# Moving two weight rests, five semaphore waits and one product order in a two-block fp32 transformer kernel

## The reference, cut to what matters

```python
for i in range(DEPTH):                                   # DEPTH = 2
    hn = rmsnorm(x, norm_mix_w[i])
    x = x + (mlstm_mixer(hn, ...) if i == 0 else window_attn_mixer(hn, ...))
    x = x + swiglu(rmsnorm(x, norm_ffn_w[i]), ffn_w_in[i], ffn_w_out[i])
...
def swiglu(h, w_in, w_out):
    gu = h @ w_in
    gate, up = gu[..., :D_FF], gu[..., D_FF:]
    return (jax.nn.silu(gate) * up) @ w_out
...
# end of window_attn_mixer: 16 query heads, 4 key-value heads
out = out / denom.transpose(0, 1, 4, 2, 3)[..., None]
return out.reshape(B, S, Hq * hd).astype(h.dtype) @ w_out
...
# second block
y_mla = (o_mla * jax.nn.silu(z_mla)) @ w_br_mla[l]
```

## Time and profile before

| | |
|---|---|
| median of 3 runs | 973.01 us (971.74 to 973.33) |
| the profiled execution | 971.56 us, span 969.7 us |
| TensorE busy | 938.5 us, 97% |
| VectorE busy | 584.7 us, 60% |
| ScalarE busy | 478.1 us, 49% |
| mean granted TensorE clock | 0.997 of full speed |
| DMA | 150.30 MB, mean 155 GB/s |

### The profile page before, as it was taken

How to read it: one execution, slowest core, us unless ns; L and a number is a source line. 1 busy time by engine, 2 the same in 40 slices (tenths; PEclk the granted TensorE clock), 3 DMA queues, 4 the chain that set the end, 5 groups by cost and what they waited for, 6 DMA issues and landing times.

```text
span 969.7 us, 13666 instructions
## 1 busy us (share of the span) xinstructions
PE 938.5 (97%) x5035; PEld 778.2 (80%) x5035; DVE 584.7 (60%) x1078; ACT 478.1 (49%) x770; POOL 24.7 (3%) x39
## 2 busy tenths in 40 slices
PE   6999899999999999899999999999999999999996
PEld 6877677888888898777888888889987877888775
DVE  5966857545454688456445454877665556565665
ACT  5556566353443548364353444686344455445442
POOL 0013200000000000000000000000000000000000
PEclk9999999999999999999999999999999999999998
DMA  8551345645546322245644546232423242433441
GB/s 296 213 195 66 134 146 217 223 168 179 210 156 234 131 87 89 87 147 199 233 157 167 222 148 240 90 130 89 173 92 126 87 164 98 174 120 131 167 169 44
DMA packets 25607, 150.30 MB, mean 155 GB/s; under 512 B 3024, under 2 KB 3152, under 8 KB 11344
## 3 DMA queue, kind: packets, MB, share of 16 engines
q1 hardware_dynamic: 24912, 147.44, 41.6%
q0 software_dynamic: 640, 2.11, 0.7%
HBM read 148.50 MB, written 1.05 MB: 154 GB/s over the span
## 4 chain that ended last, share of the span: by engine, by line
PE 83%; DVE 8%; ACT 3%; DMA 2%; issue 1%; DVEq 1%; SPq 0%; ACTq 0%
PE bank L452 24%; PE bank L453 24%; PE bank L454 23%; DVE w_lo L1803 2%; DMA w_raw<-w_main_dram 2%; PE bank L523 2%; PE bank L1008 1%; PE bank L732 1%; DVE arena L2191 1%; PE bank L1023 1%; PE bank L1061 1%; PE bank L1043 1%; PE bank L1044 1%; DVE w_lo L1782 1%; PE bank L845 1%
## 5 line engine op out<-in xcount | busy, mean ns | idle before, releaser
L452 PE MATMUL bank<-w_hi,x_hi 128*128 128x512 f32 (+2 forms) x648 | 262.4, 405 | 1.3 <-DVE w_lo L1717 0.8
L453 PE MATMUL bank<-w_lo,x_hi 128*128 128x512 f32 (+2 forms) x648 | 253.6, 391 | 0.0
L454 PE MATMUL bank<-w_hi,x_lo 128*128 128x512 f32 (+2 forms) x648 | 252.2, 389 | 0.0
L1717 DVE TENSOR_TENSOR w_lo<-w_raw,w_hi 128x2048 fp32r<-128x2048 f32 x50 | 114.6, 2292 | 106.3 <-ACT w_hi L1208 105.5
L1208 ACT ACTIVATE w_hi<-w_raw 128x2048 fp32r<-128x2048 f32 x54 | 103.4, 1917 | 105.9 <-DMA w_raw<-w_main_dram 102.2
L452 PEld LDWEIGHTS bank<-w_hi,x_hi 128*128 128x128 f32 x648 | 122.2, 189 | 32.1 <-issue 5.6
L454 PEld LDWEIGHTS bank<-w_hi,x_lo 128*128 128x128 f32 x648 | 121.7, 188 | 27.3
L453 PEld LDWEIGHTS bank<-w_lo,x_hi 128*128 128x128 f32 x648 | 122.0, 188 | 22.4
L1803 DVE TENSOR_TENSOR w_lo<-w_raw,w_hi 128x2048 fp32r<-128x2048 f32 x51 | 116.2, 2284 | 6.2 <-ACT w_hi L1269 6.1
L1269 ACT ACTIVATE w_hi<-w_raw 128x2048 fp32r<-128x2048 f32 x50 | 94.9, 1908 | 14.8 <-DMA w_raw<-w_main_dram 14.2
L452 PE MATMUL bank<-x_hi,w_hi 128*128 128x256 f32 (+1 forms) x272 | 79.7, 293 | 9.2 <-DVE w_lo L1813 8.9
(11 more groups left out here) (357 smaller groups left out, 1451.8 us busy)
## 6 DMA issues: line engine op xcount, KB each, us to landing
w_raw<-w_main_dram SPq DMA_DIRECT2D x111, 1024.0 KB, 5.4
s_raw<-w_side_dram SPq DMA_DIRECT2D x51, 512.0 KB, 4.2
w_raw<-w_main_dram SPq DMA_DIRECT2D x2, 512.0 KB, 7.1
h<-x_dram SPq DMA_DIRECT2D x2, 512.0 KB, 11.2
arena<-rows_dram POOLq DMA_DIRECT2D x2, 512.0 KB, 4.0
arena<-x_t_dram SPq DMA_DIRECT2D x1, 768.0 KB, 7.8
out_dram<-arena SPq DMA_DIRECT2D x1, 512.0 KB, 2.6
out_dram<-arena SPq DMA_DIRECT2D x2, 256.0 KB, 2.1
```

What stands on the lines that cost most here:

```text
L452: pe.matmul(out, ah, bh, start=first, stop=False)
L453: pe.matmul(out, ah, bl, start=False, stop=False)
L454: return pe.matmul(out, al, bh, start=False, stop=last)
L1717: dve.tensor_tensor(w_lo[:, slot, 4 * g:4 * g + 4, :], w_raw[:, g, :, :], w_hi[:, slot, 4 * g:4 * g + 4, :], ALU.subtract).then_inc(w_lo_o ...
```

## The change

Five edits; no instruction is added or removed but waits.

1. Start of each SwiGLU (TensorE): the wait for the second accumulator stands in front of the first product that writes it, not in front of the transposes of tile 2.
2. Head 20 of the second block (TensorE): half 0 of the rider waits for tiles 0 to 3 only; the wait for all eight stands in front of half 1.
3. Window attention (ScalarE): `w_hi` of chunk 23's second half is made behind tile 3 of the output projection, not behind tile 7.
4. Window attention (VectorE): `w_lo` of chunk 23's first half moves from in front of the third group's normalisation to behind tile 3, the second half from behind tile 7 to behind tile 5.
5. Start of each SwiGLU (VectorE): `w_lo` of the second chunk's second half stands between the two products of row blocks 0 and 1, not behind them. For this `product` calls its argument `between` behind the first.

```diff
@@ def ffn(layer, mixer, next_st), TensorE
-                for r in range(R):
-                    pe.wait_ge(acc_free[(n0 + r) % 2], (n0 + r) // 2)
+                pe.wait_ge(acc_free[n0 % 2], n0 // 2)
                 for k in range(KT - 2):
                     st_wait(f"f{layer}", k)
...
                     for r in range(R):
+                        if (k, r) == (0, 1):
+                            pe.wait_ge(acc_free[(n0 + 1) % 2], (n0 + 1) // 2)
                         first(k, r)
@@ heads of the second block, TensorE
-                if n == min(j for j in range(2 * NH) if RIDERS[j] and RIDERS[j][0][0] == "brm"):
-                    st_wait("o_mla")
+                if n == first_brm:
+                    st_wait("o_mla", KT // 2 - 1)
...
+                if n == first_brm:
+                    st_wait("o_mla")
                 riders(RIDERS[n], 1)
@@ window attention, ScalarE
                     split_st("a_out", lambda k: y_hi[:, k, :], ks=(2 * i, 2 * i + 1))
-            split_half(C_AOUT + 1, (C_AOUT + 1) % 2, 1)
+                    if i == 1:
+                        split_half(C_AOUT + 1, (C_AOUT + 1) % 2, 1)
@@ def ffn, VectorE
-                product(0)
-                rest_second(c0 + 1, (c0 + 1) % 2)
+                product(0, lambda: rest_second(c0 + 1, (c0 + 1) % 2))
@@ window attention, VectorE
-                elif j == 2:
-                    rest_half(C_AOUT + 1, (C_AOUT + 1) % 2, 0)
-            rest_st("a_out", lambda k: y_hi[:, k, :], lambda k: y_lo[:, k, :], ks=range(6))
+            rest_st("a_out", lambda k: y_hi[:, k, :], lambda k: y_lo[:, k, :], ks=range(4))
+            rest_half(C_AOUT + 1, (C_AOUT + 1) % 2, 0)
+            rest_st("a_out", lambda k: y_hi[:, k, :], lambda k: y_lo[:, k, :], ks=(4, 5))
+            rest_half(C_AOUT + 1, (C_AOUT + 1) % 2, 1)
             group_attended(NG - 1)
             rest_st("a_out", lambda k: y_hi[:, k, :], lambda k: y_lo[:, k, :], ks=(6, 7))
-            rest_half(C_AOUT + 1, (C_AOUT + 1) % 2, 1)
```

More of the change, by code:

```diff
@@ L1132, in _ @@
             evacuated(("uv", 2, 0), ("uv", 2, 1))
+            first_brm = RIDERS.index([("brm", 0, 0)])
             for n in range(2 * NH):
```

## The result

| | before | after |
|---|---|---|
| median, timed side by side | 972.75 us (971.74 to 973.33, 4 runs) | 964.27 us (963.32 to 965.36, 4 runs) |
| ratio, with its interval | | 0.9911 (0.990 to 0.9923) |
| profiled execution | 971.56 us, span 969.7 us | 965.36 us, span 963.6 us |

The change saves 8.5 us by the medians and 6.2 us between the two profiled executions. So the first question is not whether the stops went, but why more came back than they held.

What follows compares the result with a forecast made beforehand. TensorE, busy 97% of the span, was taken as the bound, so only its stops could be saved: 3.4 + 1.0 + 1.0 + 0.9 = 6.3 us off the 973.01 us median, predicting 966.7 us, range 965.0 to 969.2 us.

Steps and rivals of the forecast that it cites:

- The clock: Around the 2.4 us stop, 402 to 410 us: granted clock 1.00, so no time at a lower clock can be won back.
- The sum: All closed TensorE stops together: 3.4 + 1.0 + 1.0 + 0.9 = 6.3 us saved.
- Part 3: Second-half `w_lo` wait in each SwiGLU: both 0.49 us waits go, 1.0 us saved, with 0.2 to 0.4 us of cover.
- Part 4: Wait for turned tiles of the first branch, at 821.60 us: the 0.93 us stop is hidden, 0.9 us saved.
- Part 1: Last rests of the window attention: 1.1 us saved at 387 us and 2.3 us at 406 to 408.6, 3.4 us together.
- Part 2: Accumulator wait before each SwiGLU: 0.2 us saved in layer 0, 0.8 us in layer 1, 1.0 us together.
- 1, ScalarE's copy as the releaser: At 388.24 us TensorE waits for ScalarE's copy of head 13, so the first place gives nothing: 967.8 us; chance 0.08.
- 2, savings taken back: In the SwiGLUs, turned tiles and the late second product take savings back: 4.6 us left, 968.4 us; chance 0.14.
- 3 and 4, loads or `w_hi` late: Chunk 24's first half lands after 405: 970 to 973 us, chance 0.04; or chunk 23's `w_hi` late: 975 us, chance 0.02.
- 5, the addition kept by the meta rows: Window attention's end: the meta rows' round trip through ScalarE keeps the first addition late; 4.0 us, 969.0 us; chance 0.04.

Runs made afterwards that it cites:

- Experiment 6: Kernel before with only chunk 23's second-half `w_hi` (ScalarE) and `w_lo` (VectorE) moved earlier in the window attention: 969.04 us, 0.9958, 3.9 us faster.
- experiment 7: Kernel before with nothing moved and 18 useless identity transposes put in TensorE's 2.4 us stop: 971.72 us, 0.9984, 1.2 us faster.
- experiment 12: The kernel before again, nothing changed, for a second profile: 972.88 against 972.93 us, 0.9999.
- experiment 8: Kernel before with only `w_lo` of the second chunk's second half put between the two SwiGLU products, both layers: 971.5 us, 0.9985, 1.45 us faster.
- experiment 4: Kernel before with only TensorE's wait for turned tiles at head 20 of the second block split: 971.76 us, 0.999, 1.2 us faster.
- experiment 5: Kernel before with only VectorE's `w_lo` of chunk 23's first half moved behind tile 3: 971.48 us, 0.9982, 1.5 us faster.
- experiment 2: Kernel before with only the window attention moves, both `w_lo` halves of chunk 23 and ScalarE's `w_hi`: 967.64 us, 0.9946, 5.3 us faster.
- Experiment 10: Changed kernel with ScalarE's tile 2 and first sum of squares ahead of the two weight copies in each SwiGLU; against the kernel before: 963.84 us, 0.9901.
- experiment 9: Kernel before with only TensorE's wait for the second accumulator moved at each SwiGLU start: 971.02 us, 0.9977, 2.4 us faster.
- experiment 3: Kernel before with only both SwiGLU edits, the moved accumulator wait and the `w_lo` between the products: 968.74 us, 0.9955, 4.2 us faster.
- experiment 11: Kernel before with both SwiGLU edits and 18 useless identity transposes in the 2.4 us stop: 968.73 us, 0.9951, 4.65 us faster.

## Why the prediction was wrong

**The clock: the step that failed.** It said: "the granted clock is 1.00, the level of 2.4 GHz, so no time at a lower clock can be won back there". The row was true of one execution, and that was one of the two without the fall. In most executions, as far as five of seven profiles and the clocks on record tell, the 2.4 us stop costs a further 14.04 - 12.49 = 1.55 us behind it. I held the rule against one row and let the row decide; closing the stop wins this back. Experiment 6 (3.9 us for 2.4), experiment 7 (1.2 us faster by useless work) and experiment 12 (the fall seen) show it. The profiled execution lay 1.45 us below the median of before, and I used both numbers without asking why. That is about what one fall costs, but it proves none: experiment 12's profiled execution had the fall and still lay 0.8 us below its median, with a start 1.1 us shorter.

**The sum, mis-sized by 0.9 us.** It took each stop at the idle time in its bracket, 6.3 us; from the mark to the end, without a fall on either side, 7.2 us were saved (850.14 - 842.93). Parts 3 and 4 carry most of the rest: 1.42 us for 1.0 (experiment 8) and 1.2 us for 0.9 (experiment 4). In dense work the matmuls start 0.23 us apart while a row lasts 0.39, so a bracket, counted from the last row's end, leaves out 0.16 us of standing. And the first matmul behind a stop is followed after 0.33 us (408.12 - 407.79), not 0.23: another 0.10. By that a stop that closes entirely, between dense products, is worth its bracket and about 0.26 us. Part 1's didn't bring this, since they don't close entirely: the product at 405.37 still follows its forerunner after 0.49 us (experiment 6: 2.30 us for a bracket of 2.40), the value products stand 0.07 us behind the end of the transposes (experiment 5: 1.05 us for 1.16), and experiment 2 gave 3.35 us for both, for a forecast of 3.4. With the clock the whole is worth 7.2 us in an execution without a fall and 8.8 in one with it, and the timed 8.5 lies between.

**Part 1** was right in mechanism at both places: the value products follow the transposes at once, the 2.4 us wait is under 0.2, both `w_lo` are done before the last `group_attended`, and the moved work fits. The load of chunk 24 is issued at 393.45 and 397.94 us, the prediction's 393 and 398, and nothing waits for it.

**Part 2**: in layer 0 the prediction let 0.2 us arrive and the wait for the last tile grow from 0.25 to 0.85. It grew to 0.71, and 22.62 us from the mark to its end became 22.37: 0.25 us. Experiment 10 shows that the weights which land late on ScalarE were the cause, as the step said. In layer 1 the wait stayed (0.24 us in the profile before, 0.22 after), so the 0.8 us arrived, and some 0.1 with them: between the two turned tiles 289.02 us became 284.04, of which part 1 is 3.35 and part 3 0.65, and 0.98 are left.

**Part 3**: both waits went; the cover of 0.2 to 0.4 us held: in layer 0 the second product ends at 148.40 us, and its transposes start at 148.77.

**Part 4**: right, but for the size above.

**The rivals.** 1, ScalarE's copy as the releaser, falls by experiment 5. 2, savings taken back in both layers and by the second product, falls by experiments 8 and 9: the one wait that has grown is layer 0's, as the forecast itself had it. 3 and 4, loads or `w_hi` late, and 5, the addition kept by the meta rows, show nowhere in the profile after: the addition waits for TensorE's products. What none of them held was the case that came: that the stops cost more than they show. All my rivals took something off the sum; the clock stood in the prediction as a remark and had no chance of its own. The chances don't add up either: forecast, rivals 1, 2 and 5 and half of rival 3 make 0.96, not 0.93. Two small terms are off by 0.1 us without effect: in part 3 the second product would end at 147.6 (147.1 + 0.48), and 24 products at 0.23 are 5.5.

**Left open.** Why the clock falls in some executions and not in others, when the stop is 2.40 us in both. And the three kernels with edit 1 but without edits 3 and 4 are timed below what their profiles give against experiment 12's (851.72 us from the mark to the end): experiment 9 by 1.1 us (2.4 for 1.26), experiment 3 by 1.8 (4.2 for 851.72 - 849.28 = 2.44), experiment 11 by 0.8 (4.65 for 851.72 - 847.88 = 3.84). In the whole, beside experiments 2 and 4, edits 1 and 5 together are left with 8.6 - 5.3 - 1.2 = 2.1 us. A part has an explanation in the record: experiment 3's fastest execution and its median one (968.04 and 968.74 us) have a mean clock of 0.998, and no profile with a fall has more than 0.997, so its median most likely lacks the 1.5 us of the fall that its profile has; and 0.4 us of experiments 9 and 11 is the higher median of before in their series. What is left of experiments 9 and 11, 0.7 and 0.4 us, isn't explained. The start of the program moves by as much between executions, and no profile here shows another place for it; more profiles of one kernel weren't taken.

## What to carry to other kernels

Where TensorE is the bound, price a stop at its idle time, plus what the pipelined rows hide (here some 0.2 to 0.3 us where it closes entirely between dense products, nothing where 0.1 us of it stays), plus what the clock may cost behind it, and look for the last in more than one profile: one execution with a clock of 1.00 doesn't say that the next has it. When the profiled execution lies off the median by more than the runs scatter around it, ask for the reason before subtracting from either. For a stop of some 2 us that can't be closed, useless matmuls in it can be worth more than nothing (1.2 us here), and closing it is worth more (3.9 us).

## What the runs showed that I had not expected

A single stop of 2.40 us on a TensorE that is 97% busy was followed by about 4 us at mostly 1.2 GHz in five of seven profiles; it cost 1.5 to 1.6 us each time, and in experiment 8 it began 1 us behind the restart. Eighteen transposes of the identity, 2.13 us of work without use, held the clock at 2.4 GHz in the one profile taken with them alone, and again in experiment 11's. And the start of the program varies by some 2.8 us between profiles of kernels whose code there is the same (118.48 to 121.32 us at the mark), so spans of single profiles tell small differences only from a mark behind it.
